# A decoder layer in FP32 on one core: routing lists a row tile sooner, first expert weights requested ahead, six of eight up-projection chunks as split F32R products

## The chip, the cores and the metric

One Trainium2 chip, of which the kernel uses one core. The metric is the device time of one execution in microseconds (us); the number compared is the median of several runs.

## What is computed

One layer of a post-norm decoder trunk over 1024 tokens of width 1024, in FP32. The first half is a token mixer of four branches. The second half, where the change lies, is a mixture of experts:

```
x = layer_norm(ALPHA * x + token_mixer(x), ln1_g, ln1_b)
scores = sigmoid(x @ router_w.T)
eidx   = top 6 of scores + router_b, within the best 4 of 8 groups    # 64 experts
gate   = scores[eidx] / sum * 2.5
routed[t] = sum_e gate[t, e] * ((silu(x[t] @ wg[e]) * (x[t] @ wu[e])) @ wd[e])
shared = (silu(x @ sh_wg) * (x @ sh_wu)) @ sh_wd
x = layer_norm(ALPHA * x + routed + shared, ln2_g, ln2_b)
```

`wg[e]` and `wu[e]` are 1024x256, `wd[e]` is 256x1024. The 6144 (token, expert) pairs are grouped by expert in blocks of up to 128 rows. With these inputs 53 experts have one block and 11 have two: 75 blocks, and one empty one, since the loop runs over pairs.

## The kernel before

The second half is `back()`. It gives each engine a program of its own; semaphores tie the programs together, and every order is written out by hand.

**Routing.** For row tiles t = 0 to 7 (128 tokens each) TensorE multiplies by the output projection (`rows_out`), VectorE normalizes (`normed1`), TensorE transposes (`turn_x1`) and computes router scores (`router`), VectorE picks the six experts (`chosen`), TensorE counts ahead of each row how many earlier rows chose the same expert (`counts`, L1727 on), and VectorE turns that into six places and gates per row (`put`, L2101 on). GpSimd then writes each tile's entries to the list in memory, `slots`, with six indirect DMAs (`place_rows`, L1575). `put(n)` runs in iteration n + 4 of VectorE's loop (L2127), `counts(n)` in iteration n + 3 of TensorE's (L1802). The last tiles follow behind the loop.

**Start of the expert stage.** Sync (SP) waits until all 48 list writes have landed (L1491), reads the list back (`slots_sb`, L1492), VectorE copies two index columns (`take_idx`, L2182), GpSimd gathers the rows of blocks 0 and 1 (L1546), TensorE transposes them (`turn`, L1686). Around that the shared expert of row tiles 0 to 3 is computed. SP requests the weights of experts 2 and 3 behind the last of these row tiles' stores (L1499 to L1504).

**The block loop.** One body per block b, two bodies per trip; block b is finished while b + 1 and b + 2 are prepared.

- TensorE: two transposes of the hidden rows (L1842); `up(b + 1)`, the products with `wg` and `wu` side by side (512 columns), in 8 chunks k of 128 rows; `turn(b + 2)`, 8 transposes; `down(b)`, 12 split products (L1723).
- Chunks 0 to 3 of `up` are FP32 matmuls (L1708; the trace shows two matmul records for each). Chunks 4 to 7 are split: each operand is a high part, the value rounded to F32R, and a low part, the rest; the chunk is the three F32R products high by high, high by low, low by high (L1704 to L1706).
- ScalarE rounds: `down_high` (L1988), `up_high` (L1886, two chunks of `wg` and `wu` per instruction, 128x1024), `turned` (L1880, L1881) brings the transposed rows from PSUM, `gated` (L1891) is silu, L2008 and L2009 bring the output rows from PSUM.
- VectorE subtracts for the low parts: `down_low` (L2217), `h_lo` (L2220), `row_low` (L2210), `up_low` (L2201, L2204). `hide` (L2195) forms the hidden rows, and `take_gate`, `take_idx` and L2237 copy columns of the list.
- GpSimd gathers block b + 4 and scatters block b with an add (L1603).
- SP streams 3 MiB per expert through rings of four buffers: `step(k)` requests the up weights of expert k + 3 once `up` of expert k - 1 is done (L1429), waits until those of k + 1 have landed (L1441), requests the down weights of k + 2 (L1435), and waits for those of k (L1445).

**Last stage.** The shared expert of row tiles 4 to 7 and the second layer norm. ScalarE goes back and forth between silu (L1975), copies (L1980, `tail_turned`), square roots (L2020, `deviation`) and the normalization itself (L2024, `normal`); VectorE takes the statistics (L2303), the scale (L2282 to L2284, `scales`) and the gain (L2288). Silu and square root need different activation tables.

## Time and profile before

| | |
|---|---|
| median of 3 runs | 2051.14 us (2051.0 to 2052.28) |
| the profiled execution | 2052.17 us, its span 2050.3 us |
| TensorE (PE) busy | 1982.3 us, 97% of the span |
| VectorE (DVE) busy | 1233.8 us, 60% |
| ScalarE (ACT) busy | 858.9 us, 42% |
| GpSimd (POOL) busy | 581.2 us, 28% |
| granted TensorE clock, mean | 0.989 |
| moved by DMA | 389.59 MB |

The profile gives one row per instruction or merged group: start and duration in us, engine, line, operation, output and inputs, and in brackets how long the engine had been idle before it and what ended that. PE are matmuls and PEld weight loads. A matmul's modelled duration is longer than the distance to the next one, since they are pipelined; the distances between starts are what the engine takes. A granted clock of 1.00 is 2.4 GHz, 0.50 is 1.2 GHz. The routing stage lies at about 1050 to 1193 us, the block loop at 1220 to 1979 us.

### The profile page before, as it was taken

The page shows a single profiled execution, that of the slowest core. Times are in us where ns is not written, and L with a number is a line of the kernel's source. Part 1 is how long each engine was busy: PE and PEld are TensorE (multiplying, and loading weights), DVE is VectorE, ACT ScalarE, POOL GpSimd, SP SyncE. Part 2 cuts the span into 40 slices and gives each one's busy share as a digit, 9 for nine tenths or more (in the row PEclk, how much of TensorE's full clock was granted, in tenths as well). Part 3 has the DMA queues.
Part 4 walks back from the last instruction along what each step waited for, and adds up shares of the span by engine and source line. Part 5 has one row for each costly group of instructions (what it writes and reads, how often), then busy time and mean ns, then how long its engine had stood idle before and what let it go on. Part 6 is the DMA issues. An engine that isn't in the chain of part 4 may idle for free. (4 is left out here: it accounts for less than half of the span.)

```text
span 2050.3 us, 31214 instructions
## 1 busy us (share of the span) xinstructions
PE 1982.3 (97%) x9189; PEld 1432.5 (70%) x9190; DVE 1233.8 (60%) x2424; ACT 858.9 (42%) x1446; POOL 581.2 (28%) x406
## 2 busy tenths in 40 slices
PE   8999999999999999989999969999999999999995
PEld 7887787877778766658767537777777777777762
DVE  2794643444116777788757836666666666666646
ACT  3111221234112344450123326666666666666643
POOL 2342231333313211002122532232322232222224
PEclk9999999999999999999999989999999999999998
DMA  6123221222612210058581467999998989999956
GB/s 201 51 62 93 82 59 35 78 62 50 171 58 88 79 48 21 19 183 274 186 305 40 177 247 251 314 358 348 323 358 306 355 327 346 326 328 327 315 166 181
DMA packets 170609, 389.59 MB, mean 190 GB/s; under 512 B 27904, under 2 KB 100897, under 8 KB 145824
## 3 DMA queue, kind: packets, MB, share of 16 engines
q1 hardware_dynamic: 131312, 300.08, 40.1%
q0 software_dynamic: 30000, 71.66, 14.0%
q10 hardware_dynamic: 9216, 16.78, 2.2%
q8 instruction: 49, 0.80, 0.2%
q14 instruction: 32, 0.26, 0.0%
HBM read 337.53 MB, written 80.79 MB: 204 GB/s over the span
## 5 line engine op out<-in xcount | busy, mean ns | idle before, releaser
L644 PE MATMUL a_bank<-x_hi,w_hi 128*128 128x512 f32 x928 | 372.9, 402 | 0.0
L644 PE MATMUL a_bank<-x_hi,w_lo 128*128 128x512 f32 x928 | 362.4, 390 | 0.0
L644 PE MATMUL a_bank<-x_lo,w_hi 128*128 128x512 f32 x928 | 361.5, 390 | 0.0
L1708 PE MATMUL e_bank<-w_gu,work 128*128 x616 | 278.9, 596 | 2.2 <-issue 1.4
L579 POOL CAST w_hi<-w_raw 128x1024 fp32r<-128x1024 f32 x56 | 64.7, 1156 | 560.5 <-PE a_bank L644 539.4
L2217 DVE TENSOR_TENSOR d_lo<-w_d,d_hi 128x1024 fp32r<-128x1024 f32 x152 | 179.4, 1222 | 70.3 <-ACT d_hi L1988 70.3
L644 PEld LDWEIGHTS a_bank<-x_hi,w_hi 128*128 128x128 f32 x928 | 174.2, 188 | 40.7 <-issue 6.1
L644 PEld LDWEIGHTS a_bank<-x_hi,w_lo 128*128 128x128 f32 x928 | 174.2, 188 | 37.8
L644 PEld LDWEIGHTS a_bank<-x_lo,w_hi 128*128 128x128 f32 x928 | 174.6, 188 | 33.9 <-issue 0.5
L1708 PEld LDWEIGHTS e_bank<-w_gu,work 128*128 128x128 f32 x616 | 112.5, 193 | 114.9 <-issue 114.9
L1546 POOL DMA_INDIRECT work<-x1d,idx x78 | 80.5, 1032 | 333.4 <-DVE idx L2182 329.3
L1886 ACT ACTIVATE u_hi<-w_gu 128x1024 fp32r x150 | 159.0, 1061 | 0.7 <-issue 0.5
L1988 ACT ACTIVATE d_hi<-w_d 128x1024 fp32r x152 | 152.3, 1049 | 5.8 <-issue 3.8
L1704 PE MATMUL e_bank<-u_hi,x_g_hi 128*128 128x512 f32 x300 | 148.7, 496 | 0.0
L581 POOL TENSOR_TENSOR w_lo<-w_raw,w_hi 128x1024 fp32r<-128x1024 f32 x56 | 145.4, 2596 | 4.6
L1891 ACT ACTIVATE norm<-e_bank 128x256 f32<-128x256 f32 x76 | 29.2, 384 | 232.7 <-PE e_bank L1706 226.0
L1723 PE MATMUL e_bank<-d_hi,h_hi 128*128 128x512 f32 x304 | 125.4, 413 | 0.0
L872 ACT ACTIVATE gate_out<-a_bank 128x512 f32<-128x512 f32 x64 | 38.2, 597 | 204.6 <-PE a_bank L644 204.5
L1723 PE MATMUL e_bank<-d_hi,h_lo 128*128 128x512 f32 x304 | 120.6, 397 | 0.0
L1723 PE MATMUL e_bank<-d_lo,h_hi 128*128 128x512 f32 x304 | 119.6, 393 | 0.0
L1603 POOL DMA_INDIRECT acc<-work,idx_out x38 | 85.2, 2243 | 118.3 <-issue 112.2
L1705 PE MATMUL e_bank<-u_lo,x_g_hi 128*128 128x512 f32 x300 | 117.6, 392 | 0.0
(372 smaller groups left out, 3642.5 us busy)
## 6 DMA issues: line engine op xcount, KB each, us to landing
w_gu<-in_moe_wg SPq DMA_DIRECT2D x64, 1024.0 KB, 8.2
w_gu<-in_moe_wu SPq DMA_DIRECT2D x64, 1024.0 KB, 20.4
w_d<-in_moe_wd SPq DMA_DIRECT2D x64, 1024.0 KB, 22.0
w_raw<-in_w_in SPq DMA_DIRECT2D x53, 512.0 KB, 3.8
gates<-gate_out ACTq DMA_DIRECT2D x64, 256.0 KB, 2.0
g_sb<-gates SPq DMA_DIRECT2D x16, 1024.0 KB, 5.5
acc_odd<-zero POOLq DMA_DIRECT2D x9, 512.0 KB, 13.5
work<-in_w_out SPq DMA_DIRECT2D x4, 1024.0 KB, 8.6
```

The source lines that it names most:

```text
L579: pool.tensor_copy(w_hi[:, c % 2, :, :], w_raw[:, c % 2, :, :]).then_inc(w_hi_ready, 1)
L581: pool.tensor_tensor(w_lo[:, c % 2, :, :], w_raw[:, c % 2, :, :], w_hi[:, c % 2, :, :].bitcast(F32), ALU.subtract).then_inc(w_lo_ready, 1)
L644: ins = pe.matmul(bank[h][:, :], w[:, c % 2, k, :], x[:, k, cols], start=(k == 0 and j == 0), stop=(k == KD - 1 and j == 2))
L1546: pool.indirect_dma_start(out=x_g[:, s, :], out_offset=None, in_=x1d[:, :], in_offset=bass.IndirectOffsetOnAxis(ap=idx[:, s:s + 1], axis=0 ...
L1603: pool.indirect_dma_start(out=(acc, acc_odd)[s][:, :], out_offset=bass.IndirectOffsetOnAxis(ap=idx_out[:, s:s + 1], axis=0), in_=y_out[:, ...
L1704: pe.matmul(out, hi, u_hi[:, j, :, i, :], start=False, stop=False)
L1705: pe.matmul(out, hi, u_lo[j][:, :, i, :], start=False, stop=False)
L1708: ins = pe.matmul(out, x_gt[:, s, k, :], w_gu[:, bass.ds(e & 3, 1), :, k, :].rearrange('p a m f -> p (a m) f'), start=k == 0, stop=k == KD ...
L1723: ins = pe.matmul(bank[2 + h][:, :], x[:, j, :], w[:, j, cols], start=j == 0 and i == 0, stop=j == 1 and i == 2)
L1886: act.activation(up_part(u_hi[:, j, :, :, :]), up_weights(slot, j), ACT.Copy).then_inc(u_hi_ready, 1)
L1988: act.activation(d_hi[:, j, :], w_d[:, bass.ds(e & 3, 1), j, :].rearrange('p a f -> p (a f)'), ACT.Copy).then_inc(d_hi_ready, 1)
L2217: dve.tensor_tensor(d_lo[:, j, :], w_d[:, bass.ds(slot, 1), j, :].rearrange('p a f -> p (a f)'), d_hi[:, j, :].bitcast(F32), ALU.subtract) ...
```

## The change

Four edits.

1. `counts` and `put` each move up one row tile: `counts(t - 4)` goes inside `rows_out(t)`, between its FP32 and its split half; `put(t - 3)` takes the place of `put(t - 4)`.
2. SP requests the up weights of expert 3 as soon as row tiles 4 to 7 are stored, and the down weights of 2 and 3 before it reads the list; the up weights of expert 2 now wait until the first two gathers have landed. ScalarE scales row tiles 4 to 7 in one go, and VectorE takes the first two indices ahead of `shared_sum(2)`.
3. `PARTS` = 3: six of eight chunks of `up` are split, two (`PLAIN`) stay FP32. Per block ScalarE gets a third `up_high` and `turned` is two instructions of 256 and one of 512 columns; VectorE gets a third `up_low` and a `row_low` of 256 columns. TensorE waits per pair of chunks instead of once. The third low part lies where the zeros were, so VectorE waits once that they have been read.
4. In the last stage `deviation(4)` and `normal(3)` go ahead of `tail_turned(7)`.

```diff
+PARTS = 3
+PLAIN = KD - 2 * PARTS
...
@@ SP, start of the expert stage
             for t in range(NU, NT):
                 sp.wait_ge(x_scaled, t - NU + 1)
                 sp.dma_start(acc[t * P:(t + 1) * P, :], x1_n[:, t, :]).then_inc(acc_rest, 16)
+            sp.wait_ge(acc_rest, 16 * (NT - NU))
+            load_up(3, 3)
             for t in range(NU):
-                if t == 2:
+                if t == 1:
+                    sp.wait_ge(s_gu_done, NU)
+                    load_down(2, 2)
+                    load_down(3, 3)
                     sp.wait_ge(slots_put, 16 * NT * TOPK)
...
             sp.wait_ge(s_y, NU)
+            for k in range(2):
+                sp.wait_ge(gathered[k], 16)
             load_up(2, 2)
-            load_down(2, 2)
-            load_down(3, 3)
-            sp.wait_ge(acc_rest, 16 * (NT - NU))
-            load_up(3, 3)
...
@@ TensorE, rows_out(t)
+                if t >= 4:
+                    counts(t - 4)
...
@@ TensorE, up
-                split = part == 1 and not (isinstance(blk, int) and blk == 0)
-                if split:
-                    pe.wait_ge(u_lo_dve, 3 * blk)
+                split = not (isinstance(blk, int) and blk == 0)
                 out = bank[s][:, :].rearrange('p (m f) -> p m f', m=2)
                 for k in range(4 * part, 4 * part + 4):
-                    if split:
...
+                    if split and k >= PLAIN:
+                        j, i = divmod(k - PLAIN, 2)
+                        if i == 0:
+                            pe.wait_ge(u_lo_dve, (PARTS + 1) * (blk - 1) + j + 2)
...
@@ TensorE, row tile loop
-                if t >= 3:
-                    counts(t - 3)
                 turn_x1(t)
+            counts(NT - 4)
...
             router(NT - 2)
-            counts(NT - 4)
...
@@ ScalarE, turned
-                act.activation(x_gt[:, s, 0:4, :], bank[4][:, :].rearrange('p (k c) -> p k c', k=4), ACT.Copy)
+                act.activation(x_gt[:, s, 0:PLAIN, :], bank[4][:, 0:PLAIN * P].rearrange('p (k c) -> p k c', c=P), ACT.Copy)
+                act.activation(high[:, s, PLAIN:4, :], bank[4][:, PLAIN * P:].rearrange('p (k c) -> p k c', c=P), ACT.Copy)
...
@@ ScalarE, body
                     up_high((w >> 10) & 3, 0)
                     turned(b + 2, s)
-                    up_high((w >> 10) & 3, 1)
+                    for j in range(1, PARTS):
+                        up_high((w >> 10) & 3, j)
...
@@ ScalarE, last stage
             tail_turned(6)
+            deviation(4)
+            normal(3)
             act.wait_ge(s_down, NU + 2)
             tail_turned(7)
-            for t in range(4, NT):
+            for t in range(5, NT):
                 deviation(t)
                 normal(t - 1)
...
@@ VectorE, row tile loop and behind it
-                if t >= 4:
-                    put(t - 4)
+                if t >= 3:
+                    put(t - 3)
...
-            put(NT - 4)
             chosen(NT - 2)
...
@@ VectorE, row_low
+                dve.tensor_tensor(x_lo4[:, :, :], bank[4][:, PLAIN * P:].rearrange('p (k c) -> p k c', c=P),
+                                  x_hi[:, s, PLAIN:4, :].bitcast(F32), ALU.subtract)
...
@@ VectorE, body
+                    up_low(b + 2, (w >> 10) & 3, 0)
                     row_low(b + 2, s)
-                    up_low(b + 2, (w >> 10) & 3)
+                    for j in range(1, PARTS):
+                        up_low(b + 2, (w >> 10) & 3, j)
```

How the order stands on SP between the last store of normalized rows (`x1d`) and the loop. `w_gu` are up weights, `w_d` down weights, `acc<-work` stores of row tiles 0 to 3. Before:

```order
L1482 DMA x1d<-x 128x1024
L1429 DMA w_gu<-in_moe_wg 128x2048
L1429 DMA w_gu<-in_moe_wu 128x2048
L1435 DMA w_d<-in_moe_wd 128x2048 x2
L1488 DMA acc<-x 128x1024 x4
L1495 DMA acc<-work_49 128x1024 x2
L1492 DMA slots_sb<-slots 128x8x128
L1495 DMA acc<-work_49 128x1024 x2
L1429 DMA w_gu<-in_moe_wg 128x2048
L1429 DMA w_gu<-in_moe_wu 128x2048
L1435 DMA w_d<-in_moe_wd 128x2048 x2
```

With the change:

```order
L1488 DMA x1d<-x 128x1024
L1435 DMA w_gu<-in_moe_wg 128x2048
L1435 DMA w_gu<-in_moe_wu 128x2048
L1441 DMA w_d<-in_moe_wd 128x2048 x2
L1494 DMA acc<-x 128x1024 x4
L1435 DMA w_gu<-in_moe_wg 128x2048
L1435 DMA w_gu<-in_moe_wu 128x2048
L1506 DMA acc<-work_49 128x1024
L1441 DMA w_d<-in_moe_wd 128x2048 x2
L1503 DMA slots_sb<-slots 128x8x128
L1506 DMA acc<-work_49 128x1024 x3
```

Six MiB were requested behind the list read; four of them now stand ahead of it, and so does one store less.

How the order stands on VectorE in one body of the block loop, from the low parts of the down weights to the copy of the scatter's indices. Before:

```order
L2217 TENSOR_TENSOR d_lo_9808<-w_d_9806,d_hi_9807 128x1024
L2220 TENSOR_TENSOR h_lo_9810<-e_bank6,h_hi_9809 128x256
L2195 SCALAR_TENSOR_TENSOR norm1<-e_bank1,row_gate,norm1 128x256
L2188 COPY row_gate<-slots_sb 128x1
L2182 COPY idx<-slots_sb 128x1
L2210 TENSOR_TENSOR x_g_lo_9813<-e_bank5,x_g_hi_9812 128x512
L2201 TENSOR_TENSOR u_lo0_9814<-w_gu_9805,u_hi_9811 128x1024
L2204 TENSOR_TENSOR u_lo1_9815<-w_gu_9805,u_hi_9811 128x1024
L2237 COPY idx_out<-slots_sb 128x1
```

With the change:

```order
L2228 TENSOR_TENSOR d_lo_9808<-w_d_9806,d_hi_9807 128x1024
L2231 TENSOR_TENSOR h_lo_9810<-e_bank6,h_hi_9809 128x256
L2207 SCALAR_TENSOR_TENSOR norm1<-e_bank1,row_gate,norm1 128x256
L2200 COPY row_gate<-slots_sb 128x1
L2194 COPY idx<-slots_sb 128x1
L2213 TENSOR_TENSOR u_lo0_9815<-w_gu_9805,u_hi0_9811 128x1024
L2219 TENSOR_TENSOR x_g_lo4<-e_bank4,x_g_hi_9813 128x256
L2221 TENSOR_TENSOR x_g_lo_9814<-e_bank5,x_g_hi_9813 128x512
L2213 TENSOR_TENSOR u_lo1_9816<-w_gu_9805,u_hi1_9812 128x1024
L2213 TENSOR_TENSOR u_lo2_9821<-w_gu_9805,u_hi2 128x1024
L2250 COPY idx_out<-slots_sb 128x1
```

Two subtractions are added, and the first low part of the up weights is taken ahead of those of the rows.

## Rows read from the trace of the kernel before

**Rows 1.** Windows: the block loop from 1250 to 1950 us.

```profile
core 0: us, PE busy (x) PEld busy (x) DVE busy (x) ACT busy (x) POOL busy (x), PEclk, DMA share, GB/s
1250.00:1950.00 700.00, 700.00 (x2920) 496.39 (x2919) 451.06 (x695) 464.37 (x696) 206.16 (x139) 1.00 0.94 330
```

**Rows 2.** Timeline of TensorE over one block body.

```profile
1455.40 3.60 PE L1708 MATMUL e_bank<-w_gu,work 128*128 x8
...
1458.44 0.80 PE L1704 MATMUL e_bank<-u_hi,x_g_hi 128*128 128x512 f32 x1
...
1459.08 0.39 PE L1705 MATMUL e_bank<-u_lo,x_g_hi 128*128 128x512 f32 x1
...
1461.61 1.04 PE L1686 MATMUL e_bank<-e_const,work 128*128 128x128 f32 x8
...
1462.41 0.48 PE L1723 MATMUL e_bank<-d_hi,h_hi 128*128 128x512 f32 x1
...
1465.50 3.60 PE L1708 MATMUL e_bank<-w_gu,work 128*128 x8
```

**Rows 3.** Timeline of ScalarE in the same body.

```profile
1461.81 0.38 ACT L1891 ACTIVATE norm<-e_bank 128x256 f32<-128x256 f32 x1 [3.01 <-PE e_bank L1706]
1462.20 1.06 ACT L1886 ACTIVATE u_hi<-w_gu 128x1024 fp32r x1
...
1466.71 2.00 ACT L1988 ACTIVATE d_hi<-w_d 128x1024 fp32r x2 [0.16 <-issue]
```

**Rows 4.** Timeline of VectorE, from the end of the body before.

```profile
1460.12 0.42 DVE L2220 TENSOR_TENSOR h_lo<-e_bank,h_hi 128x256 fp32r<-128x256 f32 x1
...
1462.23 0.48 DVE L2195 SCALAR_TENSOR_TENSOR norm<-e_bank,row_gate,norm 128x256 f32<-128x256 f32 x1 [1.69 <-ACT norm L1891]
...
1464.26 0.69 DVE L2210 TENSOR_TENSOR x_g_lo<-e_bank,x_g_hi 128x512 fp32r<-128x512 f32 x1 [0.99 <-ACT x_g_hi L1881]
...
1467.14 0.15 DVE L2237 COPY idx_out<-slots_sb 128x1 int32 x1
...
1468.41 2.36 DVE L2217 TENSOR_TENSOR d_lo<-w_d,d_hi 128x1024 fp32r<-128x1024 f32 x2 [1.13 <-ACT d_hi L1988]
```

**Rows 5.** Timeline of SP at two steps, and its longest wait for up weights.

```profile
1522.54 0.33 SPq L1429 DMA_DIRECT2D w_gu<-in_moe_wg  x1
...
1530.59 0.33 SPq L1435 DMA_DIRECT2D w_d<-in_moe_wd  x1
...
1755.54 0.33 SPq L1429 DMA_DIRECT2D w_gu<-in_moe_wg  x1
...
1763.61 0.33 SPq L1435 DMA_DIRECT2D w_d<-in_moe_wd  x1
...
SPq L1441 <- DMA w_gu<-in_moe_wu: 67.7, 19, 6.4
```

**Rows 6.** Timeline from the last `put` to the first `turn`, and gathers' time to landing.

```profile
1152.82 0.98 POOL L1575 DMA_INDIRECT slots<-entry,place  x1 [5.59 <-DVE entry L2115]
...
1177.29 0.22 DVE L2115 TENSOR_SCALAR entry<-x 128x6 f32<-128x6 f32 x1
...
1191.59 1.61 POOL L1575 DMA_INDIRECT slots<-entry,place  x1 [0.30 <-issue]
...
1194.39 0.37 SPq L1492 DMA_DIRECT2D slots_sb<-slots  x1
...
1208.52 1.94 PE L1686 MATMUL e_bank<-e_const,work 128*128 128x128 f32 x8 [13.34 <-DMA work<-x1d,idx]
...
DMA to landing us min/median/max: 4.3/8.7/9.8
```

**Rows 7.** Windows: TensorE's clock right behind its longest wait.

```profile
1208.00:1214.00 6.00, 4.06 (x11) 2.66 (x12) 0.77 (x2) 2.99 (x4) 0.99 (x1) 0.50 1.02 429
```

**Rows 8.** Timeline of the last stage, ScalarE and VectorE.

```profile
2026.90 1.28 ACT L2020 ACT_TABLE_LOAD   x1
...
2028.52 0.16 DVE L2282 RECIPROCAL ln_sd<-ln_sd 128x1 f32<-128x1 f32 x1 [3.25 <-ACT ln_sd L2020]
...
2029.66 1.22 DVE L2288 TENSOR_TENSOR x<-x,w_gu 128x1024 f32<-128x1024 f32 x1 [0.71 <-ACT x L2024]
```

More of the change, by code:

```diff
@@ L1336, in back @@
         work_at, spare_at = rings_at - 4 * KD * S, rings_at + 4 * (KD * S + 2 * NT * D)
-        u_hi = nc.alloc_sbuf_tensor_at('u_hi', [P, 2, 2, 2, FE], F32R, offset=work_at + 4 * 6 * D)
+        u_hi = [nc.alloc_sbuf_tensor_at(f'u_hi{j}', [P, 2, 2, FE], F32R, offset=work_at + 4 * (6 + j) * D) for j in range(2)]
         x_hi = nc.alloc_sbuf_tensor_at('x_g_hi', [P, 2, KD, P], F32R, offset=work_at + 4 * 2 * D)
@@ L1347, in back @@
         g2, b2 = (w_gu[:, 1, 1, 4 * i:4 * i + 4, :].rearrange('p k f -> p (k f)') for i in range(2))
+        zero_at = (nc.sbuf_base + 31) // 32 * 32
         zero = sb('zero', [P, D])[:, :]
+        assert nc.sbuf_base == zero_at + 4 * D
+        u_lo.append(nc.alloc_sbuf_tensor_at('u_lo2', [P, 2, 2, FE], F32R, offset=zero_at))
+        u_hi.append(sb('u_hi2', [P, 2, 2, FE], F32R))
+        x_lo4 = sb('x_g_lo4', [P, 4 - PLAIN, P], F32R)
         slots_sb = sb('slots_sb', [P, (NT + 1) * E, 2], I32)
@@ L1695, in up @@
                     pe.wait_ge(h_ready, blk + 1)
[L1696 to L1698 removed]
+                split = not (isinstance(blk, int) and blk == 0)
                 out = bank[s][:, :].rearrange('p (m f) -> p m f', m=2)
                 for k in range(4 * part, 4 * part + 4):
[L1701 to L1704 removed]
+                    if split and k >= PLAIN:
+                        j, i = divmod(k - PLAIN, 2)
+                        if i == 0:
+                            pe.wait_ge(u_lo_dve, (PARTS + 1) * (blk - 1) + j + 2)
+                        hi, lo = x_hi[:, s, k, :], (x_lo[:, k - 4, :] if k >= 4 else x_lo4[:, k - PLAIN, :])
+                        pe.matmul(out, hi, u_hi[j][:, :, i, :], start=False, stop=False)
                         pe.matmul(out, hi, u_lo[j][:, :, i, :], start=False, stop=False)
[L1706 removed]
+                        ins = pe.matmul(out, lo, u_hi[j][:, :, i, :], start=False, stop=k == KD - 1)
                     else:
@@ L1953, in _ @@
                     shared_gated(t + 1)
-                for i in range(2 * t + NU, 2 * t + NU + 2) if t < 2 else ():
+                for i in range(NU, NT) if t == 0 else ():
                     act.activation(x1_n[:, i, :], x1_n[:, i, :], ACT.Copy, scale=ALPHA).then_inc(x_scaled, 1)
@@ L1967, in _ @@
             act.wait_ge(gu_landed, e_one + 1)
-            for j in range(2):
+            for j in range(PARTS):
                 up_high(e_one & 3, j)
@@ L2196, in hide, with up_low @@
                                          ALU.mult, ALU.mult).then_inc(h_ready, 1)
-            def up_low(blk, slot):
-                dve.wait_ge(u_hi_ready, 2 * blk - 1)
-                dve.tensor_tensor(up_part(u_lo[0]), up_weights(slot, 0), up_part(u_hi[:, 0, :, :, :]).bitcast(F32),
-                                  ALU.subtract).then_inc(u_lo_dve, 1)
-                dve.wait_ge(u_hi_ready, 2 * blk)
-                dve.tensor_tensor(up_part(u_lo[1]), up_weights(slot, 1), up_part(u_hi[:, 1, :, :, :]).bitcast(F32),
+            def up_low(blk, slot, j):
+                dve.wait_ge(u_hi_ready, PARTS * (blk - 1) + j + 1)
+                dve.tensor_tensor(up_part(u_lo[j]), up_weights(slot, j), up_part(u_hi[j]).bitcast(F32),
                                   ALU.subtract).then_inc(u_lo_dve, 1)
@@ L2243, in _ @@
             shared_sum(1)
-            shared_sum(2)
             dve.wait_ge(words_ready, 1)
@@ L2250, in _ @@
                 take_idx(k, k, slot)
+            shared_sum(2)
             for k, slot in enumerate((w & 1023, v & 1023)):
@@ L2254, in _ @@
             take_idx(2, 0, w >> 10)
-            up_low(1, v & 3)
+            dve.wait_ge(zero_in, 16 * NT + 32)
+            for k in range(2):
+                dve.wait_ge(scattered[k], 16)
+            up_low(1, v & 3, 0)
             hide(0, 0)
@@ L2259, in _ @@
             row_low(1, 1)
+            for j in range(1, PARTS):
+                up_low(1, v & 3, j)
             with dve.Fori(0, n) as i:
```

11 lines of the change are left out of this document (3 added, 8 removed).

## Prediction, made before the changed kernel was run

> **What bounds the kernel now.** I read the windows first, then the timeline of one block on each engine, then SP's, then the two ends of the expert stage. In the block loop TensorE is busy in all of 700 us while VectorE has 451 and ScalarE 464, and DMA is busy 0.94 of the time at 330 GB/s [rows 1]. One body runs from 1455.40 to 1465.50, that is 10.1 us [rows 2], and no gap stands in it: TensorE's own work is the period. But DMA is close behind: 0.94 of 10.1 us is 9.5 us of transfers per block. Before the loop TensorE stands for 13.3 us, behind GpSimd's list writes, the read of the list and a gather [rows 6]; in the last stage VectorE waits for a square root [rows 8].
>
> **Loop, TensorE.** Chunks 0 to 3, eight FP32 records, run from 1455.40 to about 1458.84, where the first split product follows a pipelined FP32 one; eight records at 0.43 are 3.44 us, 0.86 per chunk. From 1459.08 to 1461.61 there are eleven split products, 0.230 each, 0.69 per chunk [rows 2]. Turning a chunk from FP32 into three F32R products saves 0.17 us; two chunks in 75 blocks save 0.344 x 75 = 25.8 us, and the period becomes 9.75. One transition from FP32 to F32R per block there is in either kernel.
>
> **Loop, ScalarE.** It works 464/700 of 10.1, 6.7 us per block [rows 1]. Added: one `up_high` of 1.06, and two instructions of 256 columns (0.38, as silu's) for one of 512 (about 0.59): 1.2 us, 7.9 of 9.75 [rows 3]. It idled 3.0 us ahead of silu [rows 3]. Cost nothing; the cover left is some 1.4 us.
>
> **Loop, VectorE.** 6.5 us per block [rows 1], plus 1.2 (half of the 2.36 of the down weights' pair, the same size) and 0.42 (as `h_lo`, 256 columns from PSUM) [rows 4]: 8.1. What matters is its chain. Counted from silu's start (1461.81 before): `hide` at 0.4, free at 1.5, when the first `up_high` is just done [rows 3, 4]; first `up_low` to 2.6, `row_low` 0.42 + 0.69 to 3.7, two `up_low` to 6.0. The index copy starts at 6.0; the down weights' subtraction comes 1.27 behind it, as in this body, where the branch back lies between; 7.3. It ends 2.28 later, at 9.6, and `h_lo` at 10.0 [rows 4]. TensorE begins `down` 0.60 behind silu's start [rows 2, 3], now at 9.75 + 0.60 = 10.35. It holds, by 0.35 us. I cost it at nothing; ends: nothing, and 0.3 per block if each instruction and its hand-over take a little longer.
>
> **Loop, DMA.** The same bytes must pass in a shorter time: 9.5 us of transfers per 9.75. On average this fits, but one-block experts need more than the average, two-block experts less, and between them lives a reserve. SP's timeline shows the reserve: a down load stands behind the wait for the next up weights. In the two deepest places it was issued 8.05 and 8.07 us behind the up load [rows 5]; ScalarE asks for these weights one period behind that up load, so 2.0 us were left at the first, and about 1 at the second, where the up load itself was issued 0.9 late. Every block that drains the reserve now drains 0.344 more, and the head start of three periods is 1 us shorter. With 18 and 16 blocks from the last time it was full (my count by expert sizes) this is 6.2 + 1.0 - 2.0 = 5.2 and 5.5 + 1.0 - 1.0 = 5.5 us late, less some 0.4 of slack at each on VectorE: about 10 us of TensorE waiting, where there was none. Bounds: 0, if transfers go faster when asked (19 waits for up weights, the longest 6.4 us [rows 5], never reached TensorE), and 25.8, if DMA can give no more than it gave. I take 10, by the count of rows.
>
> At full share the loop's mix would move 330/0.94 = 351 GB/s [rows 1]. The Trainium skill's page "DMA: Bandwidth & Descriptors" (Bandwidth) has 425 GB/s for a 16 MB transfer on one core, and about 358 as a core's part of the HBM with both cores streaming; by 425 the weights would keep up and those 10 us would not be paid; the row speaks for less.
>
> **Start of the stage.** GpSimd issues 30 list writes from 1152.82 to 1193.2 without a pause, 8.1 us per tile [rows 6]. With `put` a tile sooner it has one tile less in hand, while the last `put`, which ends at 1177.5, does not move, since TensorE's last `counts` doesn't: 1177.5 + 8.1 = 1185.6, which is 7.5 sooner; I take 7. `counts` inside `rows_out` waits for `chosen` two iterations back; VectorE's extra `put` at t = 3 falls into waits for TensorE. The list read then follows at about 1187. What is queued behind SP's waits: the store of row tile 1 (now behind the list read, 1189, where it was ready only then), and on VectorE `shared_sum(2)`, both wanted later. The loads of experts 2 and 3, four of six MiB, no longer run beside the first gathers. These took 8.5 us from issue to `turn`; the fastest in this stretch landed in 4.3 [rows 6]: 4.2 less. TensorE has its shared expert until about 1195 (1208.52 - 13.34), so the wait becomes some 2 us, and the clock, 0.50 (1.2 GHz) for the first 5.5 us of work behind the long wait [rows 7], should not fall: 2.7 us, I take 3. Together 14; ends 8 (list only) and 17.
>
> **Last stage.** `deviation(4)` and its table load of 1.28 us [rows 8] move ahead of the wait for row tile 7's transpose, into ScalarE's idle time; copies need no other table. VectorE's waits of 3.25 and 0.71 go [rows 8]: 4.0 us. The next wait, for `tail_down(7)`, ends as VectorE arrives. Ends 2 and 5.
>
> **Sum.** -25.8 + 10 - 14 - 4 = -33.8 against the profiled execution's 2052.2: 2018.4. The median of the runs is 1.0 below that execution: **2017 us**.
>
> **Rivals.**
> 1. *The weights keep up.* No wait appears; 10 less, 2007. For it: no wait in TensorE's 700 us before. Against: the slack of 1 to 2 us. Chance 0.2.
> 2. *DMA is the bound throughout.* Each stretch of one-block experts runs at DMA's pace, waits of 20 us: 2027. For it: 0.94 was a mean, and two loads per step were late. Chance 0.2.
> 3. *VectorE's chain becomes the period*, 10.05 in place of 9.75: 75 x 0.3 = 22 of the 25.8 gone, which relieves DMA: 2052 - 4 - 18 - 1 = 2029. Chance 0.08.
> 4. *Slower than before.* VectorE and GpSimd hold each other up: the loop has a gather and a scatter by GpSimd per block, and VectorE now has a third long subtraction. If VectorE stood 1.1 us per block, its chain of 10.0 against 10.35 would give a period of 10.5: 75 x 0.4 = +30 where -25.8 was, less 18: 2063. It decides from 0.95 us per block (0.35 of slack, 0.344 of saving, 0.25 for the 18 us of the ends). Against: the pair of subtractions lasts 2.36, twice 1.18 [rows 4], though a GpSimd issue lies in every block. Chance 0.02. The Trainium skill's page "SBUF — State Buffer" (SBUF: two separate sides) says that a VectorE instruction with two SBUF inputs and a GpSimd one that reads SBUF shut each other out for a whole instruction; by this it is as likely GpSimd that waits, and a gather has two blocks of time.
> 5. *The list isn't sooner*, because 4 MiB of loads now meet the list's writes and read: the start gives 5 only: 2026. Chance 0.1.
>
> The forecast has 0.4. Its own uncertainty, 0 to 17 us of waits and 8 to 17 at the start, is what the range holds: 2004 to 2033. About 0.2% (4 us) is what a measurement can tell from no change. Faster 0.95; same 0.03 (case 3 with most of 5); slower 0.02.
>
> **What would show it.** Right: TensorE's period 9.75 in quiet stretches; waits of 1 to 5 us ahead of its FP32 or its `down` products in two or three places, with SP's down loads over 9 us behind the up loads; DMA share 0.96 or more; the wait ahead of the first `turn` under 4 us, with the clock at 1.00; VectorE's wait at the square root gone. Wrong: a period over 9.8 everywhere (VectorE), no wait at all (case 1), or list writes that still end near 1193.

## The result, and the profile after

The changed kernel takes 2038.9 us (median of four runs, one of which was disturbed at 2102 us and is left out of the ratio; the median of the other three is 2038.4); the kernel before took 2051.5 beside it. The ratio is 0.9933, 95% interval 0.9919 to 0.9947: 12.6 us less in the medians. The prediction was 2017 with a range of 2004 to 2033, so it had the direction and missed the size by 22 us.

The page of the changed kernel's profile, span and busy times:

```profile
span 2037.6 us, 32116 instructions
...
PE 1965.0 (96%) x9339; PEld 1463.1 (72%) x9340; DVE 1344.1 (66%) x2574; ACT 922.2 (45%) x1597; POOL 620.1 (30%) x406
```

The span is 12.7 us shorter than before. To see where, I cut it at the first and the last pair of transposes of the hidden rows (L1842 before, L1851 now), which begin each block body:

| stretch | before | after | gained | forecast |
|---|---|---|---|---|
| up to the first body | 1221.8 | 1218.0 | 3.8 | 14 |
| block loop, first to last body | 757.3 | 752.5 | 4.8 | 15.8 |
| behind it, to the end of the span | 71.2 | 67.1 | 4.1 | 4.0 |

**One body, quiet.** TensorE's timeline in the changed kernel, where nothing is late (L1851 opens the body, L1719 are the FP32 chunks, L1715 to L1717 the split ones, L1697 is `turn`, L1734 `down`):

```profile
1466.80 0.39 PE L1851 MATMUL e_bank<-e_const,norm 128*128 128x128 f32 x2
1467.02 1.88 PE L1719 MATMUL e_bank<-w_gu,work 128*128 x4
1468.34 0.79 PE L1715 MATMUL e_bank<-u_hi,x_g_hi 128*128 128x512 f32 x1
1468.97 0.40 PE L1716 MATMUL e_bank<-u_lo,x_g_hi 128*128 128x512 f32 x1
...
1472.92 1.05 PE L1697 MATMUL e_bank<-e_const,work 128*128 128x128 f32 x8
1473.73 0.48 PE L1734 MATMUL e_bank<-d_hi,h_hi 128*128 128x512 f32 x1
...
1476.58 0.39 PE L1851 MATMUL e_bank<-e_const,norm 128*128 128x128 f32 x2
```

1466.80 to 1476.58 is 9.78 us; the median over all bodies is 9.79 against 10.09. Four FP32 records fewer are 1.73 us less, where 1.72 was forecast: 1467.02 to 1468.97 is 1.95, and before the same stretch with eight records was 3.68 [rows 2]. The seventeen products from 1468.97 to 1472.92 take 3.95, 0.232 each, and the eleven before took 2.53 [rows 2]: the six that are new cost 1.42. So a block saves 0.31 by these rows, 0.30 by the medians, not 0.344.

**The loop's waits.** TensorE's waits from 1150 to 2050 in the changed kernel (us in total, times, longest). `x_g_hi` is ScalarE's rounding of the transposed rows, which stands behind its wait for up weights; `d_lo` is VectorE's low part of the down weights. Three of its rows:

```profile
PE e_bank L1697 <- DMA work<-x1d,idx: 8.5, 1, 8.5
PE e_bank L1719 <- ACT x_g_hi L1891: 6.3, 6, 1.9
PE e_bank L1734 <- DVE d_lo L2228: 3.7, 5, 1.2
```

SP's waits from 1200 to 2000 in the changed kernel, for up weights (L1447) and for down weights (L1451). Before, the waits for up weights were 67.7 us, 19 of them, the longest 6.4 [rows 5]:

```profile
SPq L1447 <- DMA w_gu<-in_moe_wu: 193.4, 42, 7.2
...
SPq L1451 <- DMA w_d<-in_moe_wd: 114.6, 43, 4.0
```

ScalarE at two of the late bodies of the changed kernel:

```profile
1738.89 1.06 ACT L1896 ACTIVATE u_hi<-w_gu 128x1024 fp32r x1 [2.92 <-SPq L1447]
...
1750.68 1.06 ACT L1896 ACTIVATE u_hi<-w_gu 128x1024 fp32r x1 [2.88 <-SPq L1447]
```

These waits add up to less than the cost. The distances between the starts of bodies show all of it. With the bodies counted from 0, they are over the median in three places: in bodies 22 and 23 by 2.8 us together, in 29 to 32 by 5.2, in 50 to 55 by 9.9 (each from 11.1 to 12.4 us long). Before, only the first body was over it, by 1.2, and that it still is. All places together are 18.1; 0.2 of it lies in bodies 2 and 42. Without them the loop would take 752.5 - 18.1 = 734.4 in place of 757.3: its account is 22.9 gained and 18.1 lost again.

The windows 1250 to 1950 and 1700 to 1750 of the changed kernel (PE, PEld, DVE, ACT, POOL busy, clock, DMA share, GB/s):

```profile
1250.00:1950.00 700.00, 688.48 (x3069) 526.97 (x3068) 552.00 (x837) 523.26 (x837) 242.82 (x139) 1.00 0.95 330
...
1700.00:1750.00 50.00, 45.98 (x205) 35.00 (x204) 35.06 (x55) 31.73 (x52) 14.34 (x9) 1.00 0.95 324
```

In the kernel before, the same 50 us had 345 GB/s and the next 50 had 326; but a fixed stretch of time holds other bodies in each kernel. Bodies 50 to 55, the last of the three places, in the changed kernel:

```profile
1716.84:1785.48 68.64, 61.53 (x266) 45.97 (x265) 48.97 (x75) 47.61 (x76) 18.05 (x12) 1.00 0.93 316
```

and the same bodies in the kernel before:

```profile
1727.70:1788.26 60.56, 60.56 (x254) 42.90 (x253) 39.05 (x61) 40.10 (x60) 17.59 (x12) 1.00 0.94 331
```

Over the whole loop DMA moves 330 GB/s in both [rows 1]: the loop has become only as much shorter as waits allowed. In the bodies that are latest it moves less than before, 316 against 331, while TensorE loses 7 of 69 us. It can move more: from 1350 to 1400, where nothing is late, the changed kernel has 362 GB/s at a share of 1.01. What SP waits for in bodies 50 to 55 of the changed kernel (1716 to 1785) is nearly always a landing, and hardly ever a buffer that TensorE has still to free (the third row):

```profile
SPq L1447 <- DMA w_gu<-in_moe_wu: 27.1, 5, 6.4
SPq L1451 <- DMA w_d<-in_moe_wd: 18.7, 6, 3.7
SPq L1435 <- PE e_bank L1717: 1.4, 1, 1.4
```

In the same 69 us of the kernel before (1716 to 1785) the three were 22.0, 14.6 and 12.2.

**The start.** The changed kernel's timeline there, from GpSimd's last list write to the first `turn`; the third row is SP's stores of row tiles 1 to 3, the fourth VectorE's index copies, the fifth its sum of row tile 2:

```profile
1186.73 0.98 POOL L1584 DMA_INDIRECT slots<-entry,place  x1 [0.30 <-issue]
...
1191.52 0.38 SPq L1503 DMA_DIRECT2D slots_sb<-slots  x1
...
1191.94 9.01 SPq L1506 DMA_DIRECT2D acc<-work  x3
...
1196.28 0.36 DVE L2194 COPY idx<-slots_sb 128x1 int32 x2 [6.99 <-DMA slots_sb<-slots]
...
1196.55 1.22 DVE L2154 TENSOR_TENSOR work<-work 128x1024 f32<-128x1024 f32 x1
...
1197.31 1.39 POOL L1555 DMA_INDIRECT work<-x1d,idx  x1 [9.60 <-DVE idx L2194]
...
1203.82 1.94 PE L1697 MATMUL e_bank<-e_const,work 128*128 128x128 f32 x8 [8.48 <-DMA work<-x1d,idx]
```

Against [rows 6] the writes end 5.5 us sooner, but the read goes out only 2.9 sooner: SP waits 3.8 us past the end of the last write, where it was 1.2. The gather takes 6.5 us from issue to `turn` in place of 8.5. And the granted clock fell again, to 0.50 (1.2 GHz) behind TensorE's wait of 8.5 us; windows of the changed kernel:

```profile
1196.00:1202.00 6.00, 0.00 (x0) 0.00 (x0) 2.79 (x6) 2.03 (x3) 2.41 (x2) 0.75 0.59 190
1202.00:1208.00 6.00, 2.69 (x9) 2.08 (x10) 0.15 (x1) 1.75 (x4) 0.99 (x1) 0.50 0.65 209
1208.00:1214.00 6.00, 6.00 (x10) 2.44 (x9) 1.23 (x1) 2.35 (x3) 0.00 (x0) 0.61 0.84 351
```

**The last stage** did what was forecast. ScalarE has its table load (1.28) ahead of row tile 7's copy (L1990), and the reciprocal on VectorE no longer waits, where 3.25 and 0.71 stood before [rows 8]. ScalarE in the changed kernel:

```profile
2012.14 1.28 ACT L2031 ACT_TABLE_LOAD   x1
...
2016.19 0.39 ACT L1990 ACTIVATE norm<-e_bank 128x256 f32<-128x256 f32 x1 [1.33 <-PE e_bank L1784]
```

and VectorE:

```profile
2016.59 0.11 DVE L2300 RECIPROCAL ln_sd<-ln_sd 128x1 f32<-128x1 f32 x1
...
2016.88 1.22 DVE L2306 TENSOR_TENSOR x<-x,w_gu 128x1024 f32<-128x1024 f32 x1
```

### The profile page after: what moved, and what is told of

It reads as the page before. It is cut to its first block and busy times, and to the rows that moved or that the text cites. A ratio compares the mean times of both kernels' runs of the same rounds, so it can differ in the third digit from the quotient of the medians.

```text
span 2037.6 us, 32116 instructions
## 1 busy us (share of the span) xinstructions
PE 1965.0 (96%) x9339; PEld 1463.1 (72%) x9340; DVE 1344.1 (66%) x2574; ACT 922.2 (45%) x1597; POOL 620.1 (30%) x406
## 5 line engine op out<-in xcount | busy, mean ns | idle before, releaser
L2213 DVE TENSOR_TENSOR u_lo<-w_gu,u_hi 128x1024 fp32r<-128x1024 f32 x225 | 268.3, 1220 | 42.5 <-ACT u_hi L1896 40.8
L1896 ACT ACTIVATE u_hi<-w_gu 128x1024 fp32r x225 | 230.6, 1066 | 22.4 <-SPq L1447 21.9
L1715 PE MATMUL e_bank<-u_hi,x_g_hi 128*128 128x512 f32 x450 | 208.3, 463 | 0.0
L1555 POOL DMA_INDIRECT work<-x1d,idx x78 | 111.4, 1429 | 244.3 <-DVE idx L2194 241.5
L1716 PE MATMUL e_bank<-u_lo,x_g_hi 128*128 128x512 f32 x450 | 177.8, 395 | 0.0
L1717 PE MATMUL e_bank<-u_hi,x_g_lo 128*128 128x512 f32 x450 | 177.5, 394 | 0.0
L1719 PE MATMUL e_bank<-w_gu,work 128*128 x316 | 152.9, 609 | 9.9 <-ACT x_g_hi L1891 6.3
L1612 POOL DMA_INDIRECT acc<-work,idx_out x38 | 92.2, 2427 | 142.6 <-issue 137.2
L1734 PE MATMUL e_bank<-d_hi,h_hi 128*128 128x512 f32 x304 | 125.9, 414 | 4.0 <-DVE d_lo L2228 3.7
L1734 PE MATMUL e_bank<-d_hi,h_lo 128*128 128x512 f32 x304 | 119.8, 394 | 0.0
L1734 PE MATMUL e_bank<-d_lo,h_hi 128*128 128x512 f32 x304 | 118.6, 390 | 0.0
## 6 DMA issues: line engine op xcount, KB each, us to landing
w_d<-in_moe_wd SPq DMA_DIRECT2D x64, 1024.0 KB, 25.8
acc_odd<-zero POOLq DMA_DIRECT2D x9, 512.0 KB, 13.3
```

The lines of the kernel that those rows point to most:

```text
L1555: pool.indirect_dma_start(out=x_g[:, s, :], out_offset=None, in_=x1d[:, :], in_offset=bass.IndirectOffsetOnAxis(ap=idx[:, s:s + 1], axis=0 ...
L1715: pe.matmul(out, hi, u_hi[j][:, :, i, :], start=False, stop=False)
L1716: pe.matmul(out, hi, u_lo[j][:, :, i, :], start=False, stop=False)
L1717: ins = pe.matmul(out, lo, u_hi[j][:, :, i, :], start=False, stop=k == KD - 1)
L1719: ins = pe.matmul(out, x_gt[:, s, k, :], w_gu[:, bass.ds(e & 3, 1), :, k, :].rearrange('p a m f -> p (a m) f'), start=k == 0, stop=k == KD ...
L1734: ins = pe.matmul(bank[2 + h][:, :], x[:, j, :], w[:, j, cols], start=j == 0 and i == 0, stop=j == 1 and i == 2)
```

## The experiments

Theory: the edits are worth, one by one, some 4 us (last stage), 5 (split, where waits take back 18 of 23) and 6 (list), and the loads put ahead of the list read take 2 to 3 of these away. The rivals stand with each run.

Two measures come from every trace. *Waits in the loop* are the distances between bodies over their median, summed, less the 1.2 us of the first body that every kernel has. For the start, times are counted from the issue of the last store of normalized rows (`x1d`), since the part ahead of it, which no kernel here touches, ends anywhere from 1147.3 to 1151.4 us. From there the kernel before reads the list at 45.5, has `turn` at 59.6 and the first body at 72.9; the changed one has 42.1, 54.4 and 68.6. The first body follows `turn` by 13.2 to 14.5 us in all kernels without extra products (13.3 before, and 14.5 in e1_tail, whose start is the same code), so that a difference under 1.3 us in the first body says nothing.

| run | us | ratio to before, 95% | read | gather to `turn` | first body | waits in loop |
|---|---|---|---|---|---|---|
| before | 2051.5 | | 45.5 | 8.5 | 72.9 | 0 |
| changed kernel | 2038.9 | 0.9933 (0.9919 to 0.9947) | 42.1 | 6.5 | 68.6 | 18.1 |
| e1_tail | 2047.7 | 0.9983 (0.9974 to 0.9992) | 45.5 | 8.5 | 74.4 | 0 |
| e2_split | 2044.5 | 0.9966 (0.9954 to 0.9978) | 45.5 | 8.6 | 73.2 | 16.3 |
| e3_list | 2045.1 | 0.9971 (0.9959 to 0.9983) | 40.3 | 4.5 | 65.2 | 0 |
| e4_list_loads | 2047.4 | 0.9984 (0.9975 to 0.9992) | 42.5 | 7.0 | 68.9 | 0 |
| e5_noloads | 2034.3 | 0.9913 (0.9898 to 0.9928) | 40.3 | 4.7 | 65.2 | 17.4 |
| e6_less | 2021.5 | 0.9847 (0.9832 to 0.9862) | 42.5 | 7.3 | 69.1 | 0 |
| e7_swap | 2036.5 | 0.9925 (0.9911 to 0.9938) | 42.3 | 6.3 | 68.7 | 13.6 |
| e8_warm | 2030.9 | 0.9903 (0.9888 to 0.9918) | 40.3 | 4.5 | 61.8 | 15.2 |
| e9_best | 2030.1 | 0.9893 (0.9878 to 0.9908) | 40.2 | 4.7 | 62.0 | 14.8 |
| e10_small | 2038.5 | 0.9942 (0.9927 to 0.9958) | 42.6 | 7.0 | 69.1 | 16.9 |
| e11_up3 | 2036.9 | 0.9932 (0.9918 to 0.9945) | 40.3 | 7.4 | 68.3 | 15.6 |
| e12_up3_sum | 2034.0 | 0.9901 (0.9885 to 0.9918) | 40.2 | 4.5 | 64.9 | 17.7 |
| e13_sum | 2034.6 | 0.9906 (0.9889 to 0.9922) | 42.4 | 4.4 | 65.9 | 18.6 |

### One edit at a time

**e1_tail**, on the kernel before:

```diff
             tail_turned(6)
+            deviation(4)
+            normal(3)
             act.wait_ge(s_down, NU + 2)
             tail_turned(7)
-            for t in range(4, NT):
+            for t in range(5, NT):
```

> The kernel before with edit 4 alone (ScalarE's order in the last stage). Theory: the last stage is worth what VectorE's two waits were, 4.0 us, whatever the loop does: 2051.5 - 4 = 2047.5, and the wait of 3.25 us at the square root is gone from VectorE's timeline. Rival: the 4.1 us by which the last stage of the changed kernel is shorter come from its loop having ended otherwise (the last blocks); then this kernel gains under 1 us.

Measured 2047.7, 3.4 less. VectorE's wait at the square root is gone from the trace, and the stretch behind the loop takes 67.0 us in place of 71.2. The last stage's gain is its own.

**e2_split** is the kernel before with edit 3, whose diff stands above.

> The kernel before with edit 3 alone (six of eight chunks split). Theory: the period is 9.79 in quiet stretches as in the changed kernel, 0.30 x 75 = 22.5 us less, and the weights are late by 15 to 20 us in all, since that comes from the bytes per expert and not from the start of the stage: the loop gains 3 to 8 us, 2044 to 2048. Rival: the waits come from the changed start (up weights of expert 2 requested 4 us later, behind the gathers), so that with the old start they are 5 us or fewer: 2034 or less.

Measured 2044.5, waits 16.3 us, nearly all in the same three places, period 9.79. The old start of the stage does not help the loop: the rival is out.

**e3_list** and **e4_list_loads** are the kernel before with edit 1, and with edits 1 and 2.

> The kernel before with edit 1 alone (counts and put a row tile sooner). Theory: in the changed kernel the loads put ahead of the list read held up its last writes; without them the last write is issued near 1186.5 and the read within 1.5 us of its end, 5.5 to 6.5 us sooner than before, the gathers take 8.5 us as before, beside the weights, and the first transpose starts at about 1202.5: 2045 to 2046. Rival: the last write's landing, not the loads, sets the read; then the read is again near 1191.5 and the gain is 3 us.

> The kernel before with edits 1 and 2 (list sooner, loads ahead of its read). Theory: it shows the start of the changed kernel, list read near 1191.5, first transpose near 1203.8, 3.8 us gained: 2047.5, which is 2 us behind edit 1 alone. Rival: the start of the changed kernel was slowed by edit 3 (a third rounding and a wait more before the first products), and this one gains 7 us or more: 2044.

Measured 2045.1 and 2047.4, both where the theories had them; edit 3 is not what slows the start. With the list alone the first body comes 7.7 us sooner; with the loads ahead of the read 4.0. e3_list in the same rows as above, SP's read and GpSimd's gather, and TensorE:

```profile
1187.71 0.43 SPq L1492 DMA_DIRECT2D slots_sb<-slots  x1
...
1193.99 1.06 POOL L1546 DMA_INDIRECT work<-x1d,idx  x1 [8.24 <-DVE idx L2181]
...
1198.45 1.94 PE L1688 MATMUL e_bank<-e_const,work 128*128 128x128 f32 x8 [5.07 <-DMA work<-x1d,idx]
```

The read goes out 2.0 us behind the end of the last write (1.5 or less was expected), 5.2 sooner than before, and the gather takes 4.5 us. That was better than this theory held (8.5 as before). In the kernel before, a store goes out 0.7 us behind the gather and the six MiB of weights 1.3 behind it; here they are 1.8 and 2.4 behind it. That a gather with this head start has its rows sooner is the likely reason; no run moves the head start alone.

**e5_noloads**, the changed kernel with SP's order, ScalarE's scaling and VectorE's sum as before the change, that is, without edit 2.

> The changed kernel without edit 2 (edits 1, 3 and 4; loads placed as before the change). Theory: the edits add up as measured one by one, list 6.0, split 6.6, last stage 3.4: 2051.1 - 16 = 2035, 3 to 4 us under the changed kernel, with the first block body starting near 1212.5 and the waits in the loop still 17 to 20 us. Rival: edit 2 bought the loop a head start on weights, and without it the loop's waits grow by as much as the start gains: 2039, as the changed kernel.

Measured 2034.3. The edits add up, waits are 17.4, and the first body comes 3.4 us sooner than in the changed kernel; the time is 4 to 5 us less, with intervals that overlap a little. Edit 2 bought nothing.

### The loop

**e6_less**, two further functions that SP's step calls; half of `wu` and of `wd` is not loaded, so that stale halves are multiplied:

```diff
+            def load_up_less(e, s):
...
+                sp.dma_start(w_gu[:, s, 1, 0:4, :].rearrange('p k f -> p (k f)'),
+                             d['moe_wu'][0, bass.ds(e, 1)].rearrange('a (p k) f -> p (a k f)', k=KD)[:, 0:4 * FE]
+                             ).then_inc(w_gu_in[s], 16)
...
+            def load_down_less(e, s):
...
+                sp.dma_start(w_d[:, s, 0, :],
+                             d['moe_wd'][0, bass.ds(e, 1)].rearrange('a (p k) f -> p (a k f)', k=2)[:, 0:D]
+                             ).then_inc(w_d_in[s], 16)
...
-                    load_up(k + 3, (s + 3) % 4)
+                    load_up_less(k + 3, (s + 3) % 4)
...
-                    load_down(k + 2, (s + 2) % 4)
+                    load_down_less(k + 2, (s + 2) % 4)
```

> The changed kernel with 1 MiB less of the 3 MiB of weights loaded per expert in the loop (half of each wu and wd left out, so that stale halves are used in their place). Theory: the loop's 18 us of waits are DMA giving no more bytes; with a third less, no body is over 9.9 us, the loop is 76 bodies of 9.79 less those waits, 734 in place of 752.5, and the time 2021. Rival: the waits are a hand-over between SP, ScalarE and VectorE that needs no shortage of DMA; then most of the 18 us stay and the time is 2033 or more.

Measured 2021.5 (expected 2021). No body is late, and the loop takes 734.4 us. The window of e6_less:

```profile
1700.00:1750.00 50.00, 50.00 (x224) 38.22 (x223) 40.79 (x62) 38.60 (x63) 18.30 (x10) 1.00 0.86 274
```

TensorE is busy throughout. With a third of the bytes gone all 18 us are gone: it is shown that DMA's load causes them, and that edit 3 is worth 23 us without them.

**e7_swap**, the changed kernel with SP's down load ahead of its wait for up weights:

```diff
-                if not isinstance(k, int) or k + 1 < E:
-                    up_landed((s + 1) % 4, turn + (s + 1) // 4)
                 if not isinstance(k, int) or 2 <= k < E - 2:
                     sp.wait_ge(d_blocks, blocks_until(k - 2) + 2)
                     load_down(k + 2, (s + 2) % 4)
+                if not isinstance(k, int) or k + 1 < E:
+                    up_landed((s + 1) % 4, turn + (s + 1) // 4)
```

> The changed kernel with one difference: in each step SP requests the down weights of expert k + 2 ahead of its wait for the up weights of k + 1. Theory: DMA's share is 0.98 to 1.01 where bodies are late, so a request made earlier finds no idle transfer time: within 3 us of the changed kernel, 2036 to 2042, waits in the loop 15 to 22 us. Rival: the down loads' standing behind that wait leaves DMA idle at times and costs the reserve; then waits fall under 8 us and the time is 2030 or less.

Measured 2036.5, waits 13.6. The time is within what the theory allowed, and its interval overlaps the changed kernel's; the waits are a little under its lower end. One premise of the theory was wrong: in bodies 50 to 55 of the changed kernel DMA's share is 0.93, not 0.98 to 1.01. Over the kernels with that order and those without, the waits are 13.6 and 14.8 against 15.2 to 18.6: perhaps 2 us, not settled.

**e10_small**, the changed kernel with the third `up_high` and `up_low` cut to one column in the loop; TensorE uses stale parts for that pair of chunks:

```diff
-                    for j in range(1, PARTS):
-                        up_high((w >> 10) & 3, j)
+                    up_high((w >> 10) & 3, 1)
+                    act.activation(up_part(u_hi[2])[:, 0:1, 0:1], up_weights((w >> 10) & 3, 2)[:, 0:1, 0:1], ACT.Copy).then_inc(u_hi_ready, 1)
```

and the same for VectorE's subtraction.

> The changed kernel with the third rounding and the third subtraction cut to one column in each body, so that TensorE uses stale parts for the first third of the split chunks and ScalarE and VectorE do as much for the up weights as before the change. Theory: the waits are set by the bytes DMA delivers; they stay at 14 to 19 us, less up to 1.2 us in each of the three places since VectorE's chain is that much shorter: 2035 to 2039. Rival: the third pair of long SBUF operations slows the transfers (324 GB/s between 1700 and 1750 where before it was 345); without it DMA carries 345 or more again and the waits fall under 9 us: 2030 or less.

Measured 2038.5, waits 16.9. The window of e10_small:

```profile
1700.00:1750.00 50.00, 44.67 (x192) 33.31 (x192) 28.44 (x53) 28.97 (x53) 10.48 (x8) 0.97 0.93 323
```

The waits are within the 15.2 to 18.6 of the kernels that have the third pair, and the time is the changed kernel's. So the third rounding and the third subtraction are not what makes TensorE wait. In this window DMA moves 323 GB/s, against 324 with the third pair. The Trainium skill's page "SBUF — State Buffer" (SBUF: two separate sides) says that a compute operation can't slow a DMA, and names one way in which it seems to, when VectorE keeps GpSimd from writing a DMA's descriptors; in this window the run agrees with the first. For the bodies 50 to 55 it is less clear: e10_small moves 331 GB/s there, the changed kernel 316 and the other versions with the third pair and all the bytes 317 to 325, while the bodies last as long (11.5 us against 11.4).

### The start

**e8_warm**, e5_noloads with five products more:

```diff
             pe.wait_ge(s_ht_out, NU)
+            for _ in range(5):
+                pe.matmul(bank[0][:, :], hid_t[1][:, 0, :], s_d[:, 0, 0:HALF], start=True, stop=True)
             turn(0, 0, 16)
```

> The changed kernel without edit 2, and with five extra FP32 products of 128x512 between the last shared product and the wait for the first gather; their result is written over unread. Theory: TensorE then waits under 1 us there instead of 5, the granted clock stays at 1.00 through the first up products, where it was 0.56 to 0.59 from 1196 to 1208 with the list sooner, and 4 us go: 2031 against 2035 without them. Rival: the clock falls all the same because the pauses around them are enough for it, or the extra products delay the first transpose: no gain, or 1 us lost.

Measured 2030.9. Windows of e8_warm:

```profile
1196.00:1202.00 6.00, 3.64 (x15) 1.88 (x14) 0.15 (x1) 2.00 (x4) 1.45 (x2) 1.00 0.93 324
1202.00:1208.00 6.00, 6.00 (x16) 2.65 (x15) 1.23 (x1) 2.10 (x3) 0.00 (x0) 1.00 1.01 423
```

and the same of e3_list, which has the list as soon, no extra products and a wait of 5.1 us:

```profile
1196.00:1202.00 6.00, 2.13 (x9) 1.76 (x10) 0.15 (x1) 1.08 (x2) 1.03 (x2) 0.59 0.92 307
1202.00:1208.00 6.00, 6.00 (x8) 2.47 (x9) 2.36 (x2) 2.00 (x2) 0.61 (x1) 0.56 1.00 421
```

TensorE waits 0.9 us in place of 5.3 in e5_noloads. The `turn` comes at the same time (51.1 against 51.2 there) and the first body 3.4 us sooner. What differs between is the granted clock: 1.00 (2.4 GHz) in both windows, where e3_list has 0.59 and 0.56 and e5_noloads 0.50 (1.2 GHz) in the second. In time it is 2030.9 against 2034.3, also 3.4, with intervals that overlap.

**e9_best**, e8_warm with e7_swap's order.

> The version with five extra products and the old place of the loads, and with the down weights requested ahead of the wait for up weights. Theory: the start's and the loop's gains add up; the order of requests took some 4 us of waits from the loop (14.8 us over the median against 19.3) and some 2 from the time: 2029 against 2031. Rival: those 4 us were the spread from run to run; then 2031 and waits of 17 us or more.

Measured 2030.1, waits 14.8 where e8_warm has 15.2: of the gain of e7_swap little is left, and the interval overlaps e8_warm's. It does not overlap the changed kernel's, so this version beats both kernels, the one before by 1.1%.

**e11_up3**, the changed kernel with the down loads of experts 2 and 3 moved behind the list read and the last stores, and without the wait for the gathers:

```diff
+            sp.wait_ge(acc_rest, 16 * (NT - NU))
+            load_up(3, 3)
             for t in range(NU):
                 if t == 2:
                     sp.wait_ge(slots_put, 16 * NT * TOPK)
...
             sp.wait_ge(s_y, NU)
             load_up(2, 2)
             load_down(2, 2)
             load_down(3, 3)
-            sp.wait_ge(acc_rest, 16 * (NT - NU))
-            load_up(3, 3)
```

(SP's part of the diff against e5_noloads, from which it also differs by ScalarE's and VectorE's part of edit 2).

> The changed kernel with the down weights of experts 2 and 3, 2 MiB, behind the list read as before, and the up weights of expert 3 still ahead of the last list writes. Theory: it is what is requested at 1181 and moved until 1190 that holds the last writes and the read; up weights requested at 1176.7 have landed by 1183. So the list read comes 1 to 2 us behind the last write, near 1188, and the kernel is as fast as without edit 2, 2034 to 2035. Rival: any 2 MiB beside the list writes cost, each half of the 3 to 4 us: 2037.

Measured 2036.9: both were right by halves. The read came at 40.3, as without edit 2, so it is the 2 MiB requested at 1181.5 in the changed kernel that held it. But the gather took 7.4 us and the first body came at 68.3. Something else of edit 2 slowed the gather. Between e11_up3 and e5_noloads stand the early load, ScalarE's scaling in one go and VectorE's order: in edit 2 its sum of row tile 2 comes behind the index copies, so that the store of that tile leaves at the moment of the gather (1196.62 and 1196.14 in e11_up3), where in e5_noloads it had left 3.5 us ahead of it.

**e12_up3_sum** and **e13_sum** undo VectorE's order alone, on e11_up3 and on the changed kernel:

```diff
             shared_sum(1)
+            shared_sum(2)
...
             for k, slot in enumerate((w & 1023, v & 1023)):
                 take_idx(k, k, slot)
-            shared_sum(2)
```

> As the version with the down weights behind the list read, and VectorE's sum of row tile 2 back ahead of the two index copies. Theory: what slowed its gathers (7.4 us from issue to the first transpose, 4.5 where the loads and VectorE's order are as before) is the store of row tile 2, which in VectorE's new order goes out at the same time as the gather; with the sum ahead it goes out right behind the read, the gathers take 4.5 to 5 us, the first transpose starts 51 to 51.5 us behind the last store of normalized rows in place of 53.8, and the time is 2034. Rival: the up weights of expert 3 requested early are what slows them; then 53.5 or more, and 2036 to 2037.

> The changed kernel with one difference: VectorE's sum of row tile 2 stands ahead of the two index copies, as before the change. Theory: the list read stays at 42.1 to 42.5 us behind the last store of normalized rows, held by the loads, but the gathers take about 5 us from issue in place of 6.5 to 7, and the first body starts at 66.5 to 67.5 in place of 68.6 to 69.1: 2037 to 2038. Rival: three stores in a row stand behind the read whatever VectorE does, and nothing moves: 68.6 or more, 2038.9.

Measured 2034.0 and 2034.6. The gathers take 4.5 and 4.4 us, and the first bodies come at 64.9 and 65.9. e13_sum:

```profile
1192.81 0.38 SPq L1503 DMA_DIRECT2D slots_sb<-slots  x1
...
1198.75 1.06 POOL L1555 DMA_INDIRECT work<-x1d,idx  x1 [10.01 <-DVE idx L2194]
...
1203.12 1.94 PE L1697 MATMUL e_bank<-e_const,work 128*128 128x128 f32 x8 [6.76 <-DMA work<-x1d,idx]
```

The theory for e12_up3_sum holds at each point. e13_sum gained more than was expected of it: 65.9 where 66.5 to 67.5 stood, and 2034.6 where 2037 to 2038 stood. One line of VectorE's order cost 2.6 us at `turn` and 3.4 at the first body (e11_up3 to e12_up3_sum), or 1.7 and 2.7 (changed kernel to e13_sum); in the medians it is 2.9 and 4.3, with intervals that still touch. That the store is what slows the gather, and not the sum itself, is an argument from their times: the line moves both. GpSimd's issue of the gather took 1.39 us in the changed kernel, beside the sum, and 1.06 in e13_sum, which is 0.3 of the 2.1.

With VectorE's order as it was, the loads cost little. e13_sum reads the list at 42.4, 2.1 us behind e5_noloads, has `turn` at 52.7 against 51.2, and the times are the same within their intervals, 2034.6 and 2034.3. So of the 3.2 us by which edit 2 put `turn` back, 1.7 are that one line and 1.5 the loads.

## Why the prediction missed

- **"Loop, TensorE", −25.8: right, a little large.** −22.9 (e6_less). The FP32 chunk cost 0.86 as stated; each of the six new products cost 0.237 and not 0.230, which leaves 0.15 per chunk, not 0.17.
- **"Loop, ScalarE" and "Loop, VectorE", 0: right, VectorE's by little.** With all the added work on them the period is 9.79. VectorE's chain was to end at 10.0 behind silu's start, 0.35 ahead of TensorE's `down`; it ends at 10.3 in every second body (silu at 1473.12, `h_lo` until 1483.42), and the next `down` starts at 1483.52: it held by 0.1. TensorE waits for `d_lo` five times, 3.7 us in all; cutting the third rounding and subtraction in e10_small gained nothing.
- **"Loop, DMA", +10: the failed step.** It was 18.1. The forecast had two places, 5.2 and 5.5 us, less 0.4 each. The one around 1522 is bodies 29 to 32: 5.2, near what was counted. The one around 1755 cost 9.9, and bodies 22 and 23 had been left out, 2.8. The count (blocks since the reserve was full, times 0.344, less the slack of before) assumes that DMA goes on delivering as before. In bodies 50 to 55 it moved 316 GB/s, not 331; an estimate from these rows is that the 21.7 MB moved there would have taken 3.1 us less at 331, which is most of what lies between 9.9 and 5.5. The sign that the forecast named did not come either: SP's down loads were to stand over 9 us behind the up loads, and stand 5.1 to 8.7 behind them between 1700 and 1790, since by then the up loads themselves go out late, behind the landing of down weights. The upper bound of 25.8 was not reached. Rival 2, "DMA is the bound throughout", named 20 and was the better case.
- **"Start of the stage", −14: the second failed step.** It was −3.8. *List, 7*: the writes ended 6.0 us sooner against the last store of normalized rows, but the read only 3.4, since 2 MiB of loads met the last writes; without them it is 5.2 (e3_list). *Gathers, 4.2*: 2.0, since VectorE's new order put a sum and the store of row tile 2 onto them; I had noted that store and sum as "wanted later" and costed them at nothing. With VectorE's order undone it is 4.2 (e13_sum). *Clock, 3*: nothing. It falls after a wait of 8.5 us, and after 5.1 too, where the forecast had a wait of some 2; no version without extra products had less than 5.1. Kept up, it is worth 3.4 (e8_warm). With list and gathers together the first `turn` came 5.2 us sooner against the last store of normalized rows. Of that, 0.9 went between `turn` and the first body, where e1_tail lost 1.2 with the code of before, and 0.5 went because the part ahead of that store ended later. Each of the three gains existed, and the change had none of them whole. Rival 5 named the loads' part; the store was in no rival.
- **"Last stage", −4.0: right.** −4.1 in the trace, −3.4 in the time of e1_tail.
- **The range.** Rivals 2 and 5 were priced each with all else as forecast. Both held at once: 2052.2 − 22.9 + 18.1 − 3.8 − 4.1 = 2039.5. Nothing in the profile set them against each other, so the range should have reached to their sum, 2036 by the prediction's own prices (2027 + 9), and 2.9 more by the smaller saving on TensorE. It ended at 2033.

Of the other signs named, the period of 9.75 came as 9.79, waits in three places and VectorE's wait at the square root came as forecast; DMA's share was 0.95 and not 0.96, the wait ahead of the first `turn` 8.5 us and not under 4, and the clock not 1.00.

What stays open: why DMA moves 5% less, at a share of 0.93, just where the weights are late, and so whether the lower rate causes the longer waits or comes with them. e2_split excludes the start. e10_small leaves the engines' added work open for this rate, though not for the waits. A rival that no run tests is SP's own order: it asks for the next up weights only when the down weights of the present expert have landed, so that when these are late so is the next request. That would fit the 18.7 us that it waits for them in bodies 50 to 55, with 1.4 for a free buffer; e7_swap moves the down request, not this wait. An uneven load of the 16 engines would fit too.

## What to carry to other kernels

When TensorE's period is cut in a loop whose DMA share is 0.94, price the cut by what transfers can follow: here 18 of 23 us came back as waits for weights, in twelve of 75 bodies, although the average fitted. A transfer moved out of one's way lands in another's: list what is in flight at its new place, stores included, and follow each reordered instruction to the DMA it releases. Rivals that don't exclude each other must be added up before the range is drawn.
